# The last down product, the last norm and the store of a decoder step as one stage by blocks of tokens

## The reference, cut to what matters

```
def layer_norm(x, g, b):
    mu = mean(x);  var = mean((x - mu)**2)
    return (x - mu) * rsqrt(var + 1e-5) * g + b

def swiglu(x, wg, wu, wd):
    return (silu(x @ wg) * (x @ wu)) @ wd          # 1024 -> 2816 -> 1024

h = layer_norm(ALPHA*x + 0.5*swiglu(x, ffn 0), g[0], b[0])
...                                                # projections, three attentions, mix, second norm
y = layer_norm(ALPHA*h + 0.5*swiglu(h, ffn 1), g[2], b[2])
```

## Time and profile before

| | |
|---|---|
| median of three runs | 3666.53 us (3665.11 to 3673.05) |
| profiled execution, its own time | 3673.46 us |
| span of the profiled execution | 3671.6 us, mean granted TensorE clock 0.949 |
| TensorE busy over the span | 90% |
| last matmul of the last `ups` ends | 3571.2 us |
| last product of the last `downs` added | 3600.9 us |
| first transpose of the store starts | 3650.6 us |
| last copy out of PSUM ends | 3667.7 us |

### The profile page before, as it was taken

One profiled execution on the slowest core, in us unless ns is written; L12 is line 12 of the kernel. 1 busy time (PEld: TensorE's weight loads), 2 busy tenths in 40 slices (PEclk: granted clock), 3 DMA queues, 4 the chain that ended last, 5 costly groups with the idle time before them and its releaser, 6 DMA issues. The chain is left out here.

```text
span 3671.6 us, 56105 instructions
## 1 busy us (share of the span) xinstructions
PE 3314.7 (90%) x21121; PEld 2999.5 (82%) x21121; DVE 888.4 (24%) x1581; ACT 625.5 (17%) x1163; POOL 794.6 (22%) x696
## 2 busy tenths in 40 slices
PE   5999999997988898786799899999796999999996
PEld 5999999996887798554688666666686999999995
DVE  2111111114206211555101022222314111111114
ACT  3000000002101100344000144434203000000003
POOL 0232222323120131022111111111021223233220
PEclk8999999998997899899899999999798999999998
DMA  5111111111110112210211299999311111111111
GB/s 141 35 51 40 42 49 34 49 49 29 29 44 22 41 40 67 91 48 17 52 43 43 60 297 307 300 305 303 121 29 29 34 46 50 33 51 43 37 37 55
DMA packets 328667, 293.12 MB, mean 80 GB/s; under 512 B 33640, under 2 KB 249064, under 8 KB 328048
## 3 DMA queue, kind: packets, MB, share of 16 engines
q1 hardware_dynamic: 317136, 275.93, 24.3%
q0 software_dynamic: 11424, 15.76, 1.6%
HBM read 279.34 MB, written 12.26 MB: 79 GB/s over the span
## 5 line engine op out<-in xcount | busy, mean ns | idle before, releaser
L207 PE MATMUL f_acc<-x_hi,w_hi_last 128*128 128x364 f32 x1056 | 233.5, 329 | 27.5 <-SPq L489 27.5
L165 POOL CAST w_hi_first<-w_raw_first 128x1024 fp32r<-128x1024 f32 (+1 forms) x96 | 82.9, 863 | 738.4 <-issue 301.3
L207 PE MATMUL f_acc<-x_hi,w_hi_first 128*128 128x364 f32 x1056 | 233.5, 329 | 6.9 <-SPq L489 6.9
L207 PE MATMUL f_acc<-x_lo,w_hi_last 128*128 128x364 f32 x1056 | 234.0, 330 | 0.0
L207 PE MATMUL f_acc<-x_hi,w_lo_last 128*128 128x364 f32 x1056 | 234.0, 330 | 0.0
L207 PE MATMUL f_acc<-x_hi,w_lo_first 128*128 128x364 f32 x1056 | 233.9, 330 | 0.0
L207 PE MATMUL f_acc<-x_lo,w_hi_first 128*128 128x364 f32 x1056 | 233.7, 329 | 0.0
L207 PEld LDWEIGHTS f_acc<-x_hi,w_hi_last 128*128 128x128 f32 x1056 | 184.0, 189 | 28.0 <-issue 28.0
L165 POOL CAST w_hi_last<-w_raw_last 128x1024 fp32r<-128x1024 f32 (+2 forms) x92 | 73.5, 799 | 614.2 <-PE f_acc L207 610.2
L596 DVE SCALAR_TENSOR_TENSOR br<-f_acc,br 128x1092 f32 x88 | 114.1, 1296 | 368.8 <-PE f_acc L207 368.8
L207 PEld LDWEIGHTS f_acc<-x_hi,w_hi_first 128*128 128x128 f32 x1056 | 184.0, 189 | 7.1 <-issue 7.1
(11 more groups left out here) (399 smaller groups left out, 6321.8 us busy)
## 6 DMA issues: line engine op xcount, KB each, us to landing
br<-cache_fox_k SPq DMA_DIRECT2D x256, 256.0 KB, 5.6
br<-cache_fox_v SPq DMA_DIRECT2D x256, 256.0 KB, 6.5
w_raw_first<-w_ffn_gate SPq DMA_DIRECT2D x22, 512.0 KB, 3.8
w_raw_first<-w_ffn_up SPq DMA_DIRECT2D x22, 512.0 KB, 3.8
w_raw_last<-w_ffn_gate SPq DMA_DIRECT2D x22, 512.0 KB, 3.8
w_raw_last<-w_ffn_up SPq DMA_DIRECT2D x22, 512.0 KB, 3.8
w_raw_first<-w_ffn_down SPq DMA_DIRECT2D x40, 256.0 KB, 2.9
w_raw_last<-w_ffn_down SPq DMA_DIRECT2D x40, 256.0 KB, 2.8
```

The source lines that it names most:

```text
L165: self.nc.gpsimd.tensor_copy(hi, raw).then_inc(self.high[s], 1)
L207: mm = self.nc.tensor.matmul(out[:, b, 0:width], w[s][:, k, :], x[:, k, b * width:(b + 1) * width], start=(k == 0 and first), stop=(k == k ...
```

## The change

Layer 1 gets the layout that layer 0 had. `phase_ffn` loses its last `downs` in both layers; a new `phase_norm_out` takes the place of `phase_norm(2)` and `phase_store`. It has three blocks of 384, 384 and 324 tokens, so that three chunks of 128 belong to a block (the last chunk has the 64 sample tokens). The last down product runs block by block through four PSUM banks, each of 8 groups (j) of 6 products; the mean is taken by `add_up` on GpSimd; there is one tile for the squares; the transposes of a block follow its norm, through two PSUM banks instead of four, and the weight tiles `w.raw` hold the output rows. In the class `Norm`, `scale` is now one operation over 8 rows, `shifted` applies weight and bias in place, and in the first norm a new `high_parts` (ScalarE, one cast of 8x364) makes `x_hi`, while `low_parts` is one operation.

```diff
                 ups(full * per, rest)
-                if layer == 1:
-                    downs(full, full * per + rest, rest)
...
                     ups(c, c * per, FC)
                     downs(c * per + FC, FC)
                 ups(full, full * per, rest)
-                if layer == 1:
-                    downs(full * per + rest, rest)
-        used = full * per + rest + (KD // 2 if layer == 1 else 0)
+        used = full * per + rest
         w.n = [b0 + used, b1 + used]
...
     def scale(self, dve, b):
         dve.wait_ge(self.rstd_ok, b + 1)
         dve.wait_ge(self.squared, b + 1)
+        row = self.g.res[:, :, self.cols(b)]
+        self.g.nc.vector.tensor_tensor(row, row, self.rstd[b][:].unsqueeze(1).broadcast_to([P, KD, self.width(b)]), ALU.mult)\
+            .then_inc(self.scaled, 1)
+
+    def shifted(self, act, b):
+        act.wait_ge(self.scaled, b + 1)
         for k in range(KD):
             row = self.g.res[:, k, self.cols(b)]
-            ins = self.g.nc.vector.scalar_tensor_tensor(row, row, self.gain[:, k:k + 1], self.rstd[b][:], ALU.mult, ALU.mult)
-        ins.then_inc(self.scaled, 1)
-
-    def shifted(self, act, b, dst):
-        act.wait_ge(self.scaled, b + 1)
-        for k in range(KD):
-            ins = self.g.nc.scalar.activation(dst[:, k, self.cols(b)], self.g.res[:, k, self.cols(b)], ACT.Identity,
-                                              bias=self.shift[:, k:k + 1])
-        ins.then_inc(self.high, 1)
+            ins = self.g.nc.scalar.activation(row, row, ACT.Identity, bias=self.shift[:, k:k + 1], scale=self.gain[:, k:k + 1])
+        ins.then_inc(self.normed, 1)
+
+    def high_parts(self, act, b):
+        act.wait_ge(self.normed, b + 1)
+        self.g.nc.scalar.copy(self.g.xh[:, :, self.cols(b)], self.g.res[:, :, self.cols(b)]).then_inc(self.high, 1)
 
     def low_parts(self, dve, b):
         g, c = self.g, self.cols(b)
         dve.wait_ge(self.high, b + 1)
-        for k in range(KD):
-            ins = g.nc.vector.scalar_tensor_tensor(g.xl[:, k, c], g.res[:, k, c], self.shift[:, k:k + 1],
-                                                   g.xh[:, k, c].bitcast(F32), ALU.add, ALU.subtract)
-        ins.then_inc(self.low, 1)
+        g.nc.vector.tensor_tensor(g.xl[:, :, c], g.res[:, :, c], g.xh[:, :, c].bitcast(F32), ALU.subtract).then_inc(self.low, 1)
...
-                n0.shifted(act, 0, g.xh)
-                n0.deviation(act, 1)
-                n0.shifted(act, 1, g.xh)
-                n0.deviation(act, 2)
-                n0.shifted(act, 2, g.xh)
+                n0.shifted(act, 0)
+                n0.high_parts(act, 0)
+                for b in range(1, NB):
+                    n0.deviation(act, b)
+                    n0.shifted(act, b)
+                    n0.high_parts(act, b)
...
+def phase_norm_out(g):
+    nc, io, w = g.nc, g.io, g.w
+    LEFT, BANKS, H = 2, 4, KD // 2
+    STARTS = [0, 3 * P, 6 * P, TW]
+    CHUNKS = [range(0, 3), range(3, 6), range(6, NCH + 1)]
...
+        sq = g.br[:, 8:12, :].rearrange("p a t -> p (a t)")[:, 0:KD * 3 * P].rearrange("p (k t) -> p k t", k=KD)
+        tree = g.sb(ctx, "n2_tree", [P, 4, 3 * P])
+        bank = [g.ps(ctx, f"n2_down{s}", [P, 512]) for s in range(BANKS)]
+        mean, var = g.ps(ctx, "n2_mean", [P, 512]), g.ps(ctx, "n2_var", [P, 512])
+        yt = [g.ps(ctx, f"y_t{x}", [P, H, P]) for x in range(2)]
+        y = w.raw
+        n2 = Norm(g, ctx, 2, mean, var, [sq], tree, STARTS)
...
+            @block.gpsimd
+            def _(pool):
+                n2.constants()
+                for b in range(NB):
+                    pool.wait_ge(added, KD * (b + 1))
+                    n2.add_up(pool, b)
+
+            @block.tensor
+            def _(pe):
+                def downs(b):
+                    for j in range(KD):
+                        i = b * KD + j
+                        if i >= BANKS:
+                            pe.wait_ge(added, i - BANKS + 1)
+                        for k in range(LEFT):
+                            for x, (wt, src) in enumerate(((w.hi, g.hh), (w.hi, g.hl), (w.lo, g.hh))):
+                                mm = nc.tensor.matmul(bank[i % BANKS][:, 0:n2.width(b)], wt[k][:, j, :], src[:, k, n2.cols(b)],
+                                                      start=(k == 0 and x == 0), stop=(k == LEFT - 1 and x == 2))
+                        mm.then_inc(summed, 1)
+
+                def turns(b):
+                    pe.wait_ge(n2.normed, b + 1)
+                    for c in CHUNKS[b]:
+                        n = P if c < NCH else TS
+                        for x in range(2):
+                            if c > 0:
+                                pe.wait_ge(read[x], c)
+                            for k in range(H):
+                                mm = nc.tensor.transpose(yt[x][0:n, k, :], g.res[:, x * H + k, c * P:c * P + n], g.ident[:])
+                        mm.then_inc(turned, 1)
...
+                downs(0)
+                downs(1)
+                n2.means(pe, 0)
+                downs(2)
+                n2.means(pe, 1)
+                n2.variances(pe, 0)
+                n2.means(pe, 2)
+                n2.variances(pe, 1)
+                turns(0)
+                n2.variances(pe, 2)
+                turns(1)
+                turns(2)
+
+            def halves(engine, x, copy, chunks):
+                for c in chunks:
+                    n = P if c < NCH else TS
+                    engine.wait_ge(turned, c + 1)
+                    if c >= 2:
+                        engine.wait_ge(stored[c % 2], 16 * (c // 2))
+                    copy(y[c % 2][0:n, x * H:(x + 1) * H, :], yt[x][0:n]).then_inc(read[x], 1)
+
+            @block.scalar
+            def _(act):
+                act.wait_ge(n2.ready, 2)
+                n2.square(act, 0)
+                n2.deviation(act, 0)
+                n2.square(act, 1)
+                n2.shifted(act, 0)
+                n2.deviation(act, 1)
+                n2.square(act, 2)
+                halves(act, 0, nc.scalar.copy, CHUNKS[0])
+                n2.shifted(act, 1)
+                n2.deviation(act, 2)
+                halves(act, 0, nc.scalar.copy, CHUNKS[1])
+                n2.shifted(act, 2)
+                halves(act, 0, nc.scalar.copy, CHUNKS[2])
+
+            @block.vector
+            def _(dve):
+                def add(i):
+                    b, j = divmod(i, KD)
+                    row = g.res[:, j, n2.cols(b)]
+                    dve.wait_ge(summed, i + 1)
+                    nc.vector.scalar_tensor_tensor(row, bank[i % BANKS][:, 0:n2.width(b)], 0.5, row, ALU.mult, ALU.add)\
+                        .then_inc(added, 1)
+
+                for i in range(KD + 5):
+                    add(i)
+                n2.centre(dve, 0)
+                for i in range(KD + 5, 2 * KD + 5):
+                    add(i)
+                n2.centre(dve, 1)
+                for i in range(2 * KD + 5, 3 * KD):
+                    add(i)
+                n2.invert(dve, 0)
+                n2.scale(dve, 0)
+                n2.centre(dve, 2)
+                n2.invert(dve, 1)
+                n2.scale(dve, 1)
+                halves(dve, 1, nc.vector.tensor_copy, CHUNKS[0])
+                n2.invert(dve, 2)
+                n2.scale(dve, 2)
+                halves(dve, 1, nc.vector.tensor_copy, CHUNKS[1])
+                halves(dve, 1, nc.vector.tensor_copy, CHUNKS[2])
...
+                g.hh, g.hl = (g.sb(last, f"h_{x}1", [P, FC, TW], F32R)[:] for x in ("hi", "lo"))
                 phase_ffn(g, 1)
                 g.end_phase()
-            phase_norm(g, 2, keep="result")
-            g.end_phase()
-            phase_store(g)
-            g.end_phase()
+                phase_norm_out(g)
+                g.end_phase()
```

More of the change, by code:

```diff
@@ L474, in phase_ffn @@
     with ExitStack() as ctx:
[L475 to L480, removed]
+        hh, hl = g.hh, g.hl
+        silu, hid = (g.br[:, (0, 8)[layer] + i, :] for i in range(2))
         acc = [g.ps(ctx, f"f_acc{s}_{layer}", [P, NB, 512]) for s in range(2)]
@@ L508, in _ @@
                 ups(full, full * per, rest)
-                if layer == 1:
-                    downs(full, full * per + rest, rest)
[L511 to L516, removed]
+                for s in range(rest):
+                    n = full * per + rest + (b0, b1)[s]
+                    sp.wait_ge(w.low[s], n + 1)
+                    sp.dma_start(w.raw[s][:].rearrange("p k c -> p (k c)"),
+                                 wd[(full * FC + s) * P:(full * FC + s + 1) * P, :]).then_inc(w.loaded[s], 16)
             @block.tensor
@@ L552, in _ @@
                 tiles(full * per, rest, KD)
[L553 to L557, removed]
+                for s in range(rest):
+                    w.split(pool, s, full * per + rest + (b0, b1)[s], KD)
             @block.scalar
@@ L765, in __init__ @@
         self.var_ok, self.std_ok, self.rstd_ok = (g.sem(f"n_{x}{which}") for x in ("var", "std", "rstd"))
```

(40 more changed lines are left out.)

35 lines of the change are left out of this document (8 added, 27 removed).

## The result

The changed kernel takes 3679.43 us (median of 20 runs, 3673.77 to 3684.99); the kernel before, run between them on the same chip, 3672.77 (20 runs, 3665.11 to 3678.95). The ratio is 1.0021, 95% interval 1.0014 to 1.0028: slower by 5 to 10 us, where 3.7 had been forecast. The profiled execution took 3679.1 us, its span is 3677.3, the mean granted clock 0.946.

A forecast was written before the change was run, and what follows sets the result against it. TensorE was taken to bound the kernel up to the last down product's end, then a 70 us chain through four engines. Tail +2.1 and first norm +1.6 gave +3.7: 3666.5 + 3.7 = 3670.2 us, range 3659 to 3680.

The forecast's parts named there:

- The first norm: First norm stage: new cast +2.7, `scale` and `low_parts` -1.0 each, two of three blocks pay; +1.6, bounds 0 to 2.5.
- step 13: Tail: ScalarE copies chunks ahead of `shifted(2)`, whose eight operations take 3.7 us.
- Step 6: Last norm: GpSimd's tree for block 2, after the adds, takes 5.5 us.
- Step 8: Last norm, after variance 1: deviation 0.6, reciprocal 2.56, `scale(1)` 3.36, VectorE's copy 0.7; 7.5 us with handovers.
- its own sign of failure: VectorE's one long multiply taking more than 4 us, so that each `scale` costs instead of saving.
- The half clock behind an idle: Tail: TensorE restarts at half clock after idling; 2.0, 1.3, 1.5, 1.6 and 2.8 us in norm and transposes, 9.2 together.
- Step 15: End of tail: after the last copy the same transfer as before (3.9 us), plus 0.5 for clearing semaphores, bounds 0 to 1.0.
- the clock that stays up: Rival for the tail: idle costs no clock, -11.2 us, 3659.0 at the full amount; chance 0.15.
- The clock that stays low: Rival for the tail: half clock after each gap up to the next, +9.9 us, 3680.1; chance 0.17.
- the bank stall: Down product: TensorE lacks a free bank after mean 0 and one block 2 group, and idles 3.3 us.
- A: Theory of the experiments: VectorE's one long `scale` operation keeps GpSimd's tree step out.
- my rival: Tail: blocks don't hold each other up, so transposes and copies leave the path, -3.8 - 4.5 - 1.4, 3660.5; chance 0.06.

The follow-up runs named there:

- the last kernel: Changed kernel with three transpose bank sets, last norm's `scale(0)` in eight operations, more adds before `centre(0)`, ScalarE reordered, first norm's old arithmetic: 3665.16 us, 0.9975 of before.

## Why the prediction was wrong

The forecast was +3.7 and called the same; it came out slower, at +5.7 between the profiled executions (spans) and 5 to 10 by the ratio. Its steps:

- **The first norm, +1.6 with an upper bound of 2.5, was the step that failed**: it is +5.3. I took `scale` down from 4.2 to 3.18 with the words "with GpSimd beside it", that is, I saw that they overlap and charged VectorE. The rows before show eight short operations beside the third step, and it took 1.12. Beside one long operation it is GpSimd that waits, until the operation ends. Instead of 1 us earlier, `centre(2)` came 1.2 us later than before, and block 0 pays 3.7 us where 0.8 was forecast. Changing the order alone gives back 3.1, of which 2.5 to 2.8 is this wait. The bounds were bounds of VectorE's and ScalarE's own times; none was for who else waits.
- **ScalarE's shift was taken as unchanged**, in the first norm (4.0) and in step 13 (3.7). It has one more operand by partition and takes 0.093 more an operation: 4.75 and 4.49. Leaving the weight out gives back 1.0 in the first norm.
- What is left of the first norm, 5.3 - 1.0 and less 2.5 to 2.8, is 1.5 to 1.8, the cast less what the long operations save; for that 1.6 was forecast, and it holds. One reading in it was wrong without harm: of the 3.6 us that VectorE's reciprocals wait in the earlier trace rows, 2.36 stand ahead of block 0's, so only 1.2 could cover anything of block 1.
- **Step 6** was 8.6 for 5.5, the same cause. Mean 2 and variance 1 stand behind it.
- **Step 8**: a `scale` of 3.36 was right for block 1. For block 0 it was 4.06, which the prediction had named as its own sign of failure ("more than 4 us"). It doesn't hold its own block up, but GpSimd's third step goes on only when it ends.
- The other steps up to 14 were each right within 1 us. The half clock behind an idle was right as a mechanism and priced too high: 6.1 came back of 9.2.
- **Step 15**: from the last copy to the end of the span 5.0 us where it was 3.9. I took 0.5 for it with 1.0 as bound; it was 1.1. Whether that is the clearing of the semaphores was not tried.
- Rivals: the clock that stays up did not happen; where it was made to, it gave 6.1 of 9.2. The clock that stays low did not either (variance 2 took 5.55, not 9.0). The blocks do hold each other up, and in the last kernel, where most of that is undone together with the bank stall and A, the tail is 12.8 shorter than after's; my rival had 9.7 for it alone, and its own share was not measured.

The edits show that GpSimd waits and for which operation; why it has to wait no run shows. A rule of the Trainium skill (SBUF — State Buffer, "SBUF: two separate sides" and "Who interferes with whom") fits what happened here. VectorE's second input from SBUF comes through a read interface that it shares with GpSimd, and a VectorE instruction with at most one input in SBUF doesn't contend with GpSimd (outside of the modes that use both ports). Of a VectorE instruction with two and a GpSimd instruction that reads SBUF, the one that starts first has the shared pair for its whole instruction. The traces agree at each point: the third step starts 0.41 behind the long multiply and ends 0.81 after it, near its own 0.95; in the tail the multiply starts 0.84 before GpSimd's second step ends and takes 4.06 for 3.36; `centre`, whose other operand is in PSUM, takes 3.34 beside a GpSimd step of 2.95 in the last kernel, and neither is late. By that rule the third step would have been put at the end of `scale(0)`, 903.36 for 900.39, some 3 us later. The Trainium skill (ScalarE: Activation LUTs, What ACT_TABLE_LOAD costs) gives about 93 ns for each operand by partition; measured 0.093 us. Both rules put a price on this change, and the prediction weighed neither.

## What to carry to other kernels

When eight short operations become one long one, read which engines run beside the long one, and charge it to them too: half a us saved on VectorE (3.19 for 3.67) made GpSimd's step 2.7 us longer (3.78 for 1.12), on the path. Put such an operation where the other engine is idle, or where one operand is in PSUM. In a stage that is a chain through four engines, look first at what stands ahead of the next block's work and at how many banks and output tiles there are: this tail was 3 us longer than its predecessor and, with another order, three sets of banks and one `scale` cut into eight, 10 us shorter.

## What the runs showed of the hardware that was not expected

- GpSimd's wait has the length of what is left of VectorE's operation: beside an operation of 3.38 us its step took 3.78, beside eight of 0.5 to 0.6 us 1.06 to 1.12, with nothing beside it 0.95.
- The granted clock doesn't follow from the kind of work alone. Transposes behind 5.06 us of idle, in three sets of eight with 0.68 us between them, stood at 0.50 for 7.6 us, 5.86 of them busy. The same transposes behind matmuls at 1.00 stayed at 1.00 (3.23 busy of 4.6). In the last kernel, behind 8.34 us of idle, the first eight took 1.97, sixteen more followed without a gap in 2.95, and the next eight, 0.71 later, took 1.06: between half and full clock TensorE did nothing but transposes. The rule that full clock doesn't engage for them (the Trainium skill, TensorE: Matmul & The Clock Gate, Part 4) is not borne out by these rows either.
- VectorE pays for the weight too: eight multiplies of 364 columns with weight and reciprocal took 4.16 us, with the reciprocal alone 3.67, and the one long multiply 3.19.
